# The row of maxima goes through DRAM on POOL's queue, and the backward stage's first tile is projected piece by piece

## What is computed

```
proj = x @ w_in                       # columns: 3*512 for q,k,v; then 512 gate, 256+128+32 latents
ret_out = silu(rg) * groupnorm(forward_scan + backward_scan)
q = rms_norm(cq) @ w_uq ;  kv = rms_norm(ckv) @ w_ukv
s = (q_nope k_nope + q_rope k_rope) * scale       # 8 heads, keys of the same group of tokens
p = softmax(s) ;  mla = p @ v
x = layer_norm(alpha*x + concat(ret_out, rms_norm(mla)) @ w_out)
x = layer_norm(alpha*x + experts(x))
```

## Time and profile before

| | |
|---|---|
| median of 3 runs | 3869.06 us (3867.48 to 3870.83) |
| the profiled execution, its own time | 3870.43 us |
| its span, first to last instruction | 3868.6 us |
| PE busy | 3570.4 us (92%) |
| DVE busy | 2204.0 us (57%) |
| ACT busy | 1532.9 us (40%) |
| POOL busy | 218.1 us (6%) |
| mean granted clock | 0.957 |

### The profile page before, as it was taken

How to read it: one execution, slowest core, us unless ns; L and a number is a source line. 1 busy time by engine, 2 the same in 40 slices (tenths; PEclk the granted TensorE clock), 3 DMA queues, 4 the chain that set the end, 5 groups by cost and what they waited for, 6 DMA issues and landing times. The chain is left out here.

```text
span 3868.6 us, 51496 instructions
## 1 busy us (share of the span) xinstructions
PE 3570.4 (92%) x19453; PEld 2994.1 (77%) x19453; DVE 2204.0 (57%) x3799; ACT 1532.9 (40%) x1963; POOL 218.1 (6%) x132
## 2 busy tenths in 40 slices
PE   8999979988999999999699739999999999999991
PEld 6888868865777777776577639999999999999991
DVE  5444467766777777775455454545545555545545
ACT  2111144434666666665322213333333333333335
POOL 0000000001000000000011101000000000001100
PEclk9999989998999999999799859999999999999995
DMA  3111155655211222200433134555555555555546
GB/s 120 60 60 60 61 171 205 222 214 112 54 41 19 54 54 54 55 6 7 154 135 130 71 101 134 166 172 159 170 166 157 159 177 158 174 162 157 169 124 242
DMA packets 314711, 470.46 MB, mean 122 GB/s; under 512 B 79072, under 2 KB 215008, under 8 KB 311904
## 3 DMA queue, kind: packets, MB, share of 16 engines
q1 hardware_dynamic: 302816, 426.94, 35.1%
q0 software_dynamic: 11776, 41.95, 5.1%
HBM read 352.83 MB, written 116.00 MB: 121 GB/s over the span
## 5 line engine op out<-in xcount | busy, mean ns | idle before, releaser
L63 PE MATMUL psum<-xeT_hi,w_hi 128*128 128x320 f32 x2048 | 635.4, 310 | 0.0
L64 PE MATMUL psum<-xeT_lo,w_hi 128*128 128x320 f32 x2048 | 633.7, 309 | 0.0
L65 PE MATMUL psum<-xeT_hi,w_lo 128*128 128x320 f32 x2048 | 633.7, 309 | 0.0
L1930 ACT ACTIVATE w_hi<-w_raw 128x2048 fp32r<-128x2048 f32 x192 | 358.6, 1907 | 295.3 <-PE psum L65 199.5
L2008 DVE TENSOR_TENSOR w_lo<-w_raw,w_hi 128x2048 fp32r<-128x2048 f32 x192 | 432.2, 2284 | 40.0 <-ACT w_hi L1930 40.0
L1243 ACT ACTIVATE p_hi<-psum 128x1024 fp32r<-128x1024 f32 x272 | 279.1, 1026 | 359.8 <-PE psum L65 359.7
L1290 DVE TENSOR_REDUCE mx<-psum 128x1 f32<-128x1024 f32 x256 | 312.8, 1224 | 168.3 <-PE psum L1167 168.3
L63 PEld LDWEIGHTS psum<-xeT_hi,w_hi 128*128 128x128 f32 x2048 | 385.4, 188 | 1.0
L64 PEld LDWEIGHTS psum<-xeT_lo,w_hi 128*128 128x128 f32 x2048 | 385.3, 188 | 0.6
L65 PEld LDWEIGHTS psum<-xeT_hi,w_lo 128*128 128x128 f32 x2048 | 385.3, 188 | 0.0
L1308 DVE TENSOR_TENSOR p_lo<-p_raw,p_hi 128x1024 fp32r<-128x1024 f32 x272 | 333.2, 1225 | 82.8 <-ACT p_raw L1245 79.5
(11 more groups left out here) (323 smaller groups left out, 6833.8 us busy)
## 6 DMA issues: line engine op xcount, KB each, us to landing
w_raw<-in_w_gate SPq DMA_DIRECT2D x64, 1024.0 KB, 6.1
w_raw<-in_w_up SPq DMA_DIRECT2D x64, 1024.0 KB, 7.6
w_raw<-in_w_down SPq DMA_DIRECT2D x64, 1024.0 KB, 5.4
rec<-rec SPq DMA_DIRECT2D x20, 768.0 KB, 3.6
recb<-rec SPq DMA_DIRECT2D x20, 768.0 KB, 5.0
xa<-in_x SPq DMA_DIRECT2D x20, 512.0 KB, 4.5
xb<-in_x SPq DMA_DIRECT2D x20, 512.0 KB, 6.1
xo<-in_x SPq DMA_DIRECT2D x20, 512.0 KB, 3.4
```

The source lines that it names most:

```text
L63: pe.matmul(out, a[0], b[0], start=first, stop=False)
L64: pe.matmul(out, a[0], b[1], start=False, stop=False)
L65: return pe.matmul(out, a[1], b[0], start=False, stop=last)
L1930: a.activation(w_hi[n % 4][:], raw[n % 4][:], ACT.Copy).then_inc(s["hi_made"], 1)
```

## The change

In the backward stage: six buffers instead of three for the raw pieces, two of them borrowed from `rec[1]` and `x[1]`; SP issues all the pieces before `rec` and tile 1; tile 0 of x is split before the weights; and PE multiplies tile 0 with each piece as soon as it is split (`project_first`), the gate in bank 2 and the latents in bank 3 side by side. The slot's own products are left out for u = 0.

In attention: POOL writes `mx4` to DRAM, waits until it has landed, and reads it back as one row into `qT_hi`; both DMAs are issued on POOL's own queue. The keys' constant row becomes -1 instead of 1, and nothing is scaled. `turn_row` and `take_row` are gone from PE and ACT. `AHEAD` becomes 14.

```diff
+        raw = [krT[:, 0:W], krT[:, W:2 * W], raw_more[0][:], raw_more[1][:],
+               rec[1][:].rearrange("p a h e -> p (a h e)")[:, 0:W], x[1][:, 0:W]]
+        for k in range(NRAW):
+            buf = k if k < 6 else k - 6 if k < DK else k % 3
+            raw_before.append(max((m + 1 for m in range(k) if raw_of[m] == buf), default=0))
...
                 load_x(0)
+                for k in range(DK):
+                    load_raw(k)
                 load_rec(0)
-                load_raw(0)
-                load_raw(1)
-                load_raw(2)
+                sp.wait_ge(s["w_lo_made"], 6)
                 load_x(1)
-                for k in range(3, DK):
-                    load_raw(k)
...
+                def project_first():
+                    pe.wait_ge(s["x_hi_made"], 1)
+                    pe.wait_ge(s["x_lo_made"], 1)
+                    for k in range(DK):
+                        pe.wait_ge(s["w_lo_made"], k + 1)
+                        x_k, first, last = (x_hi[0][:, k, :], x_lo[0][:, k, :]), k == 0, k == DK - 1
+                        gate_ins = mm3(pe, ps[:, 2, :], x_k, (w_hi[:, k, 0:RW], w_lo[:, k, 0:RW]), first, last)
+                        lat_ins = mm3(pe, ps[:, 3, 0:LAT], x_k, (w_hi[:, k, RW:W], w_lo[:, k, RW:W]), first, last)
...
+                turn(0)
+                project_first()
                 pe.wait_ge(s["state_zeroed"], 1)
-                turn(0)
-                pe.wait_ge(s["w_lo_made"], DK)
...
+                take_x_hi(0)
                 for k in range(DK):
                     split_hi(k)
-                    if k == 1:
-                        take_x_hi(0)
...
-    AHEAD = 12
+    AHEAD = 14
...
                     if j % 8 == 0:
-                        pe.wait_ge(s["row_made"], block_no(g) + 1)
+                        n = block_no(g)
+                        pe.wait_ge(row_in[n % 2], 16 * (n // 2 + 1))
...
-                    if g in row_slot:
-                        turn_row(row_slot[g])
...
+                def turn_row(n):
+                    _, h, qb = starts[n]
+                    dst = qT[h % 2][0][KQ:KQ + 1, 512 * qb:512 * (qb + 1)].bitcast(F32).rearrange("o (q p) -> o q p", q=4)
+                    by_tile = d["max_row"][n % 2].rearrange("(p q) -> q p", q=4).unsqueeze(0)
+                    g.wait_ge(s["mx4_made"], n + 1)
+                    g.dma_start(d["max_row"][n % 2].rearrange("(p q) -> p q", q=4), mx4[n % 2][:].bitcast(F32)
+                                 ).then_inc(row_out[n % 2], 16)
+                    g.wait_ge(row_out[n % 2], 16 * (n // 2 + 1))
+                    g.dma_start(dst, by_tile, allow_slow_non_contiguous=True).then_inc(row_in[n % 2], 16)
...
-                        wait_from_one(v, s["row_turned"], m - 1)
+                        if m >= 2:
+                            v.wait_ge(row_out[m % 2], 16 * (m // 2))
```

More of the change, by code:

```diff
@@ L474, in retention_backward_phase @@
     cq_hi, cq_lo, ckv_hi, ckv_lo, krT = latents
-    PREP0 = 5
+    PREP0, NRAW = 5, 14
     LAST = NT + 5
@@ L485, in retention_backward_phase @@
         uq_hi, uq_lo = sb("uq_hi", [P, 2, D], F32R), sb("uq_lo", [P, 2, D], F32R)
-        raw_last = sb("wb_stage", [P, W])
+        raw_more = [sb(f"wb_stage{b}", [P, W]) for b in range(2)]
         x = [sb(f"xb{b}", [P, D]) for b in range(2)]
@@ L521, in retention_backward_phase @@
         ret_out = [c.sem(f"b_ret_out{b}") for b in range(2)]
-        raw_in = [c.sem(f"b_raw_in{b}") for b in range(3)]
+        raw_in = [c.sem(f"b_raw_in{b}") for b in range(6)]
         kr_out = [c.sem(f"b_kr_out{b}") for b in range(2)]
@@ L749, in _ @@
                         wait_from_one(pe, s["gated"], u)
-                        project_gate(u, 0)
+                        if u >= 1:
+                            project_gate(u, 0)
                     if prep:
                         prepare(u, "V")
-                    if now:
+                    if now and u >= 1:
                         project_gate(u, 1)
@@ L771, in _ @@
                         wait_from_one(pe, s["kr_turning"], u)
-                        project_lat(u, 0)
+                        if u >= 1:
+                            project_lat(u, 0)
                     if prep:
                         prepare(u, "Q")
-                    if now:
+                    if now and u >= 1:
                         project_lat(u, 1)
@@ L1084, in attention_phase @@
         mx, den = sb("mx", [P, 8]), sb("den", [P, 4])
-        mx4 = [sb(f"mx4_{b}", [P, 4]) for b in range(2)]
+        mx4 = [sb(f"mx4_{b}", [P, 4], F32R) for b in range(2)]
         hi_in = [c.sem(f"m_hi_in{b}") for b in range(2)]
@@ L1089, in attention_phase @@
         o_out = [c.sem(f"m_o_out{b}") for b in range(2)]
-        names = ("constant_rows scored hi_made raw_made lo_made mixed unit_scored unit_reduced mx4_made row_turned row_made "
+        names = ("constant_rows scored hi_made raw_made lo_made mixed unit_scored unit_reduced mx4_made "
                  "oT_made out_turned den_made o_made").split()
         s = {n: c.sem("m_" + n) for n in names}
+        row_out = [c.sem(f"m_row_out{b}") for b in range(2)]
+        row_in = [c.sem(f"m_row_in{b}") for b in range(2)]
         NBH = NB * MH
@@ L1100, in attention_phase @@
         out_slot = {g0 + (8 if qb < 4 else 2): n for n, (g0, h, qb) in enumerate(starts)}
-        bank7 = []
-        for g in range(-AHEAD, TOTAL + 1):
-            if g in row_slot:
[L1104 to L1113, removed]
         def unit_bank(n):
@@ L1133, in load, with store_out @@
                                      ).then_inc(v_in[b], 16)
+                def store_out(n):
+                    g0, h, qb = starts[n]
+                    sp.wait_ge(s["o_made"], n + 1)
+                    sp.dma_start(d["o"][4 * qb:4 * qb + 4, :, h, :].rearrange("t p e -> p t e"), o[n % 2][:]
+                                 ).then_inc(o_out[n % 2], 16)
                 load(0)
@@ L1206, in mix @@
                     ins.then_inc(s["mixed"], 1)
-                def turn_row(n):
-                    pe.wait_ge(s["mx4_made"], n + 1)
-                    wait_bank7(pe, "row", n)
-                    for q in range(4):
-                        ins = pe.matmul(ps[0:1, 7, q * P:(q + 1) * P], mx4[n % 2][:, q:q + 1], c.ident,
-                                        start=True, stop=True)
-                    ins.then_inc(s["row_turned"], 1)
                 def turn_out(n):
                     pe.wait_ge(s["oT_made"], n + 1)
-                    wait_bank7(pe, "out", n)
+                    wait_from_one(pe, s["o_made"], n)
                     for q in range(4):
@@ L1270, in _ @@
                 for b in range(2):
-                    for part, value in ((kT[b][0][KQ:KQ + 1, :], 1.0), (kT[b][1][KQ:KQ + 1, :], 0.0),
+                    for part, value in ((kT[b][0][KQ:KQ + 1, :], -1.0), (kT[b][1][KQ:KQ + 1, :], 0.0),
                                         (qT[b][1][KQ:KQ + 1, :], 0.0), (vals[b][0][:, :, MV:MV + 1], 1.0),
@@ L1276, in _ @@
                         n += 1
+                def turn_row(n):
[7 more added lines that the diff above has]
+                    g.dma_start(dst, by_tile, allow_slow_non_contiguous=True).then_inc(row_in[n % 2], 16)
+                for n in range(len(starts)):
+                    turn_row(n)
             @block.vector
```

37 lines of the change are left out of this document (15 added, 22 removed).

## The result

| | |
|---|---|
| before, median of 4 runs beside the changed kernel | 3869.36 us (3867.48 to 3870.83) |
| with the change, median of 4 runs | 3900.22 us (3899.01 to 3904.64) |
| ratio | 1.008, 95% interval 1.0068 to 1.0093 |
| span of the profiled execution | 3898.7 us, before 3868.6 |
| mean granted clock | 0.949, before 0.957 |

The change makes the kernel 31 us slower. The forecast was 48 us faster, 3821 us in a range of 3811 to 3848, so the sign was wrong too.

A forecast was written before the change was run, and what follows sets the result against it. PE was taken to set the end of attention and of the backward stage from its second tile on. The terms -11.5 - 44.1 + 3.9 + 3.4 = -48.3 us led to a forecast of 3821 us, range 3811 to 3848.

The forecast's parts named there:

- so I take L = 12 there: Attention, rows beside a head's operand loads: L of 12 us, fitting steady blocks by 0.7, costing +3.4 at the first block.
- L: Attention: the row's way through DRAM, from `mx4` to the second DMA's landing; taken as 8 us, against 12.7 of room.
- rival A: Attention, beside loads: L is 16, six blocks wait 3.3 us each, the first 4 more; 3845 or 3855 us; chance 0.16.
- The clock behind a wait: Attention, rival A: each of six waits also lowers PE's clock, costing a further 1.7 us.
- Rival B: Attention, first scores: L exceeds 12.7 in all 31 blocks, at 15.6 costing 2.9 us each; 3914 us; chance 0.09.
- the upper end: Attention, the row's two DMAs: POOL pays per piece as for a gather, write 1.9 + 2.0, read 7.7 + 2.0, together 13.6 us.
- The turned rows: Attention, PE: 39 rows in full slots no longer turned, 1.13 us each, -44.1 us.
- Two more units: Attention, before the first score: +4.8 us, less 2 x 0.46 for units the slots no longer hold, +3.9 us.
- The backward stage: Backward stage: tile 1's gate product starts at about 523 instead of 534.92, 11.5 us gained, bounds 8 and 14.
- a shift at its start should live to its end: Backward stage from its second tile: PE busy 320.67 of 336.10 us, so the 11.5 us gained at the start should last.
- Rival C: Backward stage: DVE sets the pace in the first three tiles, the 11.5 us are lost; 3832 to 3833 us; chance 0.07.
- the first block's wait: Attention, first block: the row has 8.6 us of room and takes 12, so it costs +3.4 us.

## Why the prediction was wrong

- **The step that failed is "so I take L = 12 there".** Beside a load L was 21 us, in six blocks and at the first one 18. The step took the crowd's price, 2 to 3 us, from the gathers of the expert stage. But around the gathers of the earlier trace rows SP hands over two transfers of 1 MB and then none for 14 us, as the timeline of SP before shows below; in attention it hands over 4.5 MB at once. The DMA engines were full in both places (a share of 1.01 to 1.06 from 2478 to 2484 us, 1.00 to 1.03 from 1027 to 1042), so the share did not tell them apart. What the runs showed in its place: beside a load each of the row's two DMAs is late, the write by 7 to 8 us and the read by 6 to 7, and most of that passes before its first packet. Why the gathers fared better is not shown; the smaller amount waiting, 2 MB, is the likely reason. A row that hinted at the size was in the earlier trace rows: `v_lo` landed 20.3 us after its issue, of which its own 640 KB are some 3 at the 200 GB/s of that stretch. I used it for rival A and took L = 16 from it, without adding the delay up for two DMAs.

```profile
2476.13 0.37 SPq L1800 DMA_DIRECT2D w_raw<-in_w_gate  x1
2478.24 0.37 SPq L1800 DMA_DIRECT2D w_raw<-in_w_up  x1
2492.10 0.37 SPq L1800 DMA_DIRECT2D w_raw<-in_w_gate  x1
```

- **The clock behind a wait was named as rival A's second price, at 1.7 us; it is 2.4 to 2.9.** The wait of the earlier trace rows was 3.9 us, these are 8 to 9, and PE does most or all of a slot at 1.2 GHz after each.
- **Rival A had the mechanism, the place and the six heads right**, and its time, 3845 to 3855, wrong by 50 us for the same size of L. Against it I had set "the gathers between weight loads stayed near 8 us", which is the failed step once more. Rival B (every row late) did not happen: away from loads L was 7.4 us, a little under the 8 I took, between the ends of 4.0 and 13.6. POOL was busy 0.57 us for the write and 1.10 for the read, far from the 1.9 and 7.7 of the upper end. The Trainium skill's rule against a strided last dimension ("DMA: Bandwidth & Descriptors", "Rules for kernel authors"), cited for that end, bears on the read alone: its 4-byte elements land in 4.8 us, where the write of 16-byte rows takes 1.8, and that is half of the 9.7 the upper end gave it. The 2.0 us plus bytes from the Trainium skill's anatomy of a DMA (same page) fits the write and not the read.
- **The turned rows were worth what the sum said**: 43.9 against 44.1 us. **Two more units** cost 3.2 against 3.9.
- **The backward stage gave 8.3 to 8.7 us against 11.5**, inside its bounds of 8 to 14. PE's first piece and tile 1 came as worked out: 534.92 less the prediction's own 523 is 11.9, not the 11.5 it wrote, and 12.05 was measured. What failed is "a shift at its start should live to its end": 3.8 us went again, in stretches at a lower clock. Rival C, DVE setting the pace, is excluded by the 10.5 us at slot 2, and the same at slot 3. Of the two halves, the order of the loads carries 6.9 us.
- **The rest of the sum was right once the loads are out of the way**: its 3821 us stand against 3826.10 for that kernel. Not term by term: the backward part gave 3 us less than forecast, and the first block's wait was 1.1 us there, not 3.4.

## What to carry to other kernels

Before a small transfer is put on the path, list what every queue hands over in the same microseconds. Here a 2 KB DMA beside a queued load of 4.5 MB took 9 to 12 us on an empty queue, and 18 to 19 behind a 128 KB store in its own; a chain of two pays for each. Find the stretches with a large load from the timeline of DMA issues, not from median landings or the busy share, and move the load (here to just behind the row) before adding lead: that cost nothing and gave 74 us. Price a wait of PE of several microseconds at its length plus the work it then does at half clock.

## What the runs showed of the hardware

- The row's write, a DMA of 2 KB, landed 1.8 us after its issue (the median) and 9.8 beside a 4.5 MB load, 6.3 of them before its first packet. On SP's queue, empty, beside loads that POOL had handed over in full, it took 12.4, and 18.4 behind a store in SP's own queue.
- Small transfers overtook large ones that had been issued before them: with the queues exchanged the row's write at the first block landed before eight transfers of the load, the last of them 18 us later.
- Plain DMAs occupied POOL for 0.57 us (128 pieces of 16 bytes) and 1.10 us (512 pieces of 4), against 1.85 for a gather of 128 rows; the same two took SP 0.34 and 0.63.
- Handing over the last of a head's transfers held SP for 15.35 us, and POOL for 1.33.
- After a wait of 8.25 us PE ran a whole slot, 14 matmuls, at 1.2 GHz before the clock was back; behind the other five waits of 7.8 to 9.1 us the slot took 5.6 to 6.1 us.
